# Expert results of a turn: one indirect scatter of 4 KB pieces where two of 2 KB stood

## What is computed

```python
def hier_moe(h, w_rg, w_re, w_gate, w_up, w_down):
    ...
    eid = g_top[:, None] * EXPERTS_PER_GROUP + top_i        # 2 of 16 experts for each token
    comb = jnp.sum(jax.nn.one_hot(eid, N_EXPERTS) * wts[..., None], axis=1)
    act = jax.nn.silu(jnp.einsum('nd,edf->nef', xf, w_gate)) * jnp.einsum('nd,edf->nef', xf, w_up)
    act = act * comb.astype(act.dtype)[..., None]
    return jnp.einsum('nef,efd->nd', act, w_down).reshape(b, t, dm)
```

## Time and profile before

| what | value |
|---|---|
| median of 3 runs | 1653.67 us (1653.02 to 1654.21) |
| the profiled execution's own time | 1659.17 us |
| its span, first to last instruction | 1657.3 us |
| TensorE's mean granted clock | 0.92 of full speed |
| PE busy | 1447.2 us, 87% |
| DVE busy | 387.6 us, 23% |
| ACT busy | 296.5 us, 18% |
| POOL busy | 83.2 us, 5% |
| DMA | 380.28 MB, mean 229 GB/s |

### The profile page before, as it was taken

The page is one execution under the profiler, slowest core; times in us unless marked ns, Lnnn a source line. Parts: engine busy times, 40 slices in busy tenths (PEclk is TensorE's granted clock), DMA queues, the critical chain, the costliest instruction groups (busy, mean ns, idle before and its releaser), DMA issues. The chain is left out here.

```text
span 1657.3 us, 19981 instructions
## 1 busy us (share of the span) xinstructions
PE 1447.2 (87%) x7384; PEld 790.8 (48%) x7385; DVE 387.6 (23%) x972; ACT 296.5 (18%) x667; POOL 83.2 (5%) x111
## 2 busy tenths in 40 slices
PE   7999999999999988878899999769999888797880
PEld 4444445556788756644454575433333223232330
DVE  3101010000365265466210213520101001010015
ACT  3000000011333234357100113100000000000001
POOL 0000000000200000000000000001010100101000
PEclk9999999999999689979899999969999889998995
DMA  9376224352242077400933123979999999999965
GB/s 356 112 306 241 102 99 132 105 173 102 102 153 64 23 219 235 149 13 1 356 117 122 82 102 107 403 271 389 391 415 387 396 408 408 416 412 405 417 294 194
DMA packets 113809, 380.28 MB, mean 229 GB/s; under 512 B 17459, under 2 KB 55387, under 8 KB 83047
## 3 DMA queue, kind: packets, MB, share of 16 engines
q1 hardware_dynamic: 108050, 343.27, 54.5%
q0 software_dynamic: 5552, 27.89, 4.9%
q10 hardware_dynamic: 144, 8.26, 1.2%
HBM read 394.60 MB, written 26.49 MB: 254 GB/s over the span
## 5 line engine op out<-in xcount | busy, mean ns | idle before, releaser
L2356 PE MATMUL bank<-ring,hT_e 128*64 x576 | 267.9, 626 | 56.2 <-DMA W<-in_w_exp_up 54.6
L2357 PE MATMUL bank<-W,hT_e 128*64 128x512 f32 x576 | 267.9, 626 | 0.0
L2356 PEld LDWEIGHTS bank<-ring,hT_e 128*64 128x64 f32 x576 | 82.0, 145 | 234.8 <-issue 234.8
L2373 PE MATMUL bank<-W,const 128*64 128x512 f32 x576 | 134.3, 621 | 9.8 <-ACT const L2401 9.8
L490 PE MATMUL bank<-raw,hT 128*128 128x512 f32 (+1 forms) x320 | 134.0, 581 | 0.6 <-PEq L243 0.6
L490 PE MATMUL bank<-w_in,hT 128*128 128x512 f32 (+2 forms) x320 | 123.7, 547 | 0.0
L1712 PE MATMUL bank<-W,mixT 128*128 128x512 f32 x256 | 113.4, 604 | 1.6 <-DVE mixT L1947 1.6
L490 PEld LDWEIGHTS bank<-raw,hT 128*128 128x128 f32 x320 | 62.4, 197 | 69.0 <-issue 68.7
L490 PEld LDWEIGHTS bank<-w_in,hT 128*128 128x128 f32 x320 | 60.4, 190 | 61.0 <-issue 60.9
L2419 DVE SCALAR_TENSOR_TENSOR gate<-bank,row_w,gate 64x512 f32<-64x512 f32 x18 | 13.6, 756 | 322.1 <-ACT gate L2399 322.1
L2373 PEld LDWEIGHTS bank<-W,const 128*64 128x64 f32 x576 | 42.7, 142 | 88.0 <-issue 88.0
(11 more groups left out here) (403 smaller groups left out, 1755.3 us busy)
## 6 DMA issues: line engine op xcount, KB each, us to landing
ring<-in_w_exp_gate SPq DMA_DIRECT2D x76, 1024.0 KB
W<-in_w_exp_down SPq DMA_DIRECT2D x76, 1024.0 KB, 29.3
W<-in_w_exp_up SPq DMA_DIRECT2D x72, 1024.0 KB
raw<-in_w_in SPq DMA_DIRECT2D x3, 4096.0 KB
W<-in_w_out SPq DMA_DIRECT2D x3, 4096.0 KB, 13.5
w_in<-in_w_in SPq DMA_DIRECT2D x2, 4096.0 KB, 14.7
k_in<-in_cache_sel_k SPq DMA_DIRECT2D x64, 128.0 KB
v_in<-in_cache_sel_v SPq DMA_DIRECT2D x64, 128.0 KB, 3.4
```

Source lines behind the costliest of these rows:

```text
L2356: pe.matmul(bank[4 + u][0:NS, :], hT[:, u, c, :], w_g[:, c, :], start=(c == 0), stop=(c == KC - 1))
L2357: mm = pe.matmul(bank[4 + u][UP, :], hT[:, u, c, :], w_u[:, c, :], start=(c == 0), stop=(c == KC - 1))
L2373: mm = pe.matmul(bank[2 * u + n // 2][lane, :], actT[:, q, :], w_d[:, u, q, 512 * n:512 * n + 512], start=(q == 0), stop=(q == 3))
```

## The change

The four 512-column quarters are placed otherwise in PSUM: n = 0 and 1 now lie on partitions 0 to 63 in the two banks, n = 2 and 3 on partitions 64 to 127. Each partition half then holds 1024 adjacent columns of the row in `y`, and one scatter of 128 pieces of 4 KB writes them. The scratch is viewed in rows of 1024 floats, the row numbers are 2 in place of 4 to a pair, the table `rows_at` loses a column, and the scatter's semaphore counts 16 a turn in place of 32. The place table `lane` loses its second column, so that the constants' row is 2950 floats wide in place of 2951.

```diff
-        "place1": np.stack([4 * ((k * TILES + r) * P + p) + 1 for r in range(TILES) for k in range(2)], 1),
+        "place1": np.stack([2 * ((k * TILES + r) * P + p) + 1 for r in range(TILES) for k in range(2)], 1),
-        "lane": np.stack([p // NS - 1, p // NS + 1], 1),
+        "lane": (p // NS - 1)[:, None],
...
-                    for h in range(2):
-                        dve.scalar_tensor_tensor(out=rows_at[:, :, 1 + h], in0=table[:, 1, :], scalar=cst("lane")[:, h:h + 1], in1=blank[:, :],
-                                                 op0=ALU.add, op1=ALU.add)
+                    dve.scalar_tensor_tensor(out=rows_at[:, :, 1], in0=table[:, 1, :], scalar=cst("lane"), in1=blank[:, :],
+                                             op0=ALU.add, op1=ALU.add)
...
-            y = const[:, P:P + 2048].rearrange("p (u h n) -> p u h n", u=2, h=2)
+            y = const[:, P:P + 2048].rearrange("p (u n) -> p u n", u=2)
...
-                    sp.wait_ge(y_stored, n * 64)
+                    sp.wait_ge(y_stored, n * 32)
...
-                    y_rows = scratch["moe_y"].rearrange("r (n c) -> (r n) c", c=512)
+                    y_rows = scratch["moe_y"].rearrange("r (n c) -> (r n) c", c=1024)
...
-                        pool.wait_ge(y_stored, turn * 32)
-                        pool.tensor_copy(to_row[:, u, :], rows_at[:, bass.ds(turn, 1), 1:3].rearrange("p o c -> p (o c)")).then_inc(to_ready, 1)
+                        pool.wait_ge(y_stored, turn * 16)
+                        pool.tensor_copy(to_row[:, u:u + 1], rows_at[:, bass.ds(turn, 1), 1]).then_inc(to_ready, 1)
...
-                        for h in range(2):
-                            pool.indirect_dma_start(out=y_rows, out_offset=bass.IndirectOffsetOnAxis(ap=to_row[:, u, h:h + 1], axis=0),
-                                                    in_=y[:, u, h, :], in_offset=None, bounds_check=8 * TILES * P - 1, oob_is_err=False).then_inc(y_stored, 16)
+                        pool.indirect_dma_start(out=y_rows, out_offset=bass.IndirectOffsetOnAxis(ap=to_row[:, u:u + 1], axis=0),
+                                                in_=y[:, u, :], in_offset=None, bounds_check=4 * TILES * P - 1, oob_is_err=False).then_inc(y_stored, 16)
...
-                            for n in range(4):
-                                lane = slice(NS * (n % 2), NS * (n % 2) + NS)
-                                mm = pe.matmul(bank[2 * u + n // 2][lane, :], actT[:, q, :], w_d[:, u, q, 512 * n:512 * n + 512], start=(q == 0), stop=(q == 3))
+                            for n in (0, 2, 1, 3):
+                                lane = slice(NS * (n // 2), NS * (n // 2) + NS)
+                                mm = pe.matmul(bank[2 * u + n % 2][lane, :], actT[:, q, :], w_d[:, u, q, 512 * n:512 * n + 512], start=(q == 0), stop=(q == 3))
...
-                        act.wait_ge(y_stored, turn * 32)
-                        act.copy(y[:, u, 0, :], bank[2 * u]).then_inc(y_copied_a, 1)
+                        act.wait_ge(y_stored, turn * 16)
+                        act.copy(y[:, u, 0:512], bank[2 * u]).then_inc(y_copied_a, 1)
...
-                        dve.wait_ge(y_stored, turn * 32)
-                        dve.tensor_copy(y[:, u, 1, :], bank[2 * u + 1]).then_inc(y_copied_d, 1)
+                        dve.wait_ge(y_stored, turn * 16)
+                        dve.tensor_copy(y[:, u, 512:1024], bank[2 * u + 1]).then_inc(y_copied_d, 1)
```

More of the change, by code:

```diff
@@ L1570, in trunk @@
         ahead = sb(top, "ahead", [1, TURNS_MAX + 2], I32)
-        rows_at = sb(top, "rows_at", [P, TURNS_MAX + 2, 3], I32)
+        rows_at = sb(top, "rows_at", [P, TURNS_MAX + 2, 2], I32)
         row_w = sb(top, "row_w", [P, TURNS_MAX + 2])
@@ L2241, in trunk @@
             from_row = side("from_row", [P, 2], I32)
-            to_row = side("to_row", [P, 2, 2], I32)
+            to_row = side("to_row", [P, 2], I32)
             to_ready = sem("e_to_ready")
```

## The result

The changed kernel is **slower**: its time against the kernel before is 1.0038 of it, 95% interval 1.0027 to 1.005, from 18 runs of each (medians 1663.49 and 1656.97 us). On the 1653.67 us of the forecast that is 6.3 us more, 1660.0 us. The forecast was 1652.4 us, with a range of 1650.6 to 1654.4.

The account below looks back on a forecast made before the run. The prediction took DMA engine time to bound the experts from 1120 to 1598 us. Scatters -0.2, POOL 0, router -0.15 and tail -0.95 summed to -1.3 us: 1653.67 to 1652.4 us, range 1650.6 to 1654.4.

Parts of the forecast that it names:

- What bounds the kernel: Experts, 1120 to 1598 us: all 16 DMA engines are full (busy share 1.01, 405 GB/s), so their time bounds this stretch.
- DMA engine time of the scatters: Scatters of all turns, 5120 KB: larger pieces save 0.2 us of DMA engine time, between 0 and 0.48.
- the upper end, 0: Scatters' DMA engine time: pieces travel one to a packet of 4 KB as now, so the gain is 0.
- The gather's price: Scatters' DMA engine time: at the gather's 63.4 ns a KB the scatters would cost 7.4 us more.
- POOL a turn: Each turn: gather issued 1.32 us earlier, landing 0 to 1.32 earlier; PE's 4.6 us of gather waits nearly vanish; time gain 0.
- Router's end: Router's end, before POOL's first gather: one of two L2231 instructions on DVE goes, -0.15 us.
- Tail: After DVE's last copy: one scatter issued 1.31 us sooner than the second, its doubled data 0.35 us longer, -0.95 us.
- PE, ACT, DVE in the turn: Within each turn: same steps, banks and copy shapes, SP waits for the same events, constants' row one float shorter: 0.
- The slower rival: DMA engines, 1120 to 1598 us: 4 KB pieces dearer or slowing loads beside them, 7.4 us longer, 1660.0 us; chance 0.05.
- my three signs of being wrong: Full stretch changes over 2 us; scatter leaves 38 to 41 ns a KB; last copy to reading back doesn't shrink 0.5 to 1.3.

## Why the prediction was wrong

*What bounds the kernel:* right. The experts are bound by DMA engine time from 1120 to 1598 us. The share is 1.01 in both kernels, and that is just why 0.7 ns a KB on the loads costs some 7 us.

*DMA engine time of the scatters, -0.2 us:* the number of packets and their price did not change (128 data packets, 40.2 and 40.0 ns a KB), so the upper end, 0, is the nearer one. The gather's price, the other bound, did not come in.

*POOL a turn, 0:* right in the sum, but the step's detail was not. The gather is issued 1.3 us earlier but lands 0.1 earlier, so PE's waits for it did not shrink to nearly nothing: they are 5.5 us, where they were 4.6. A gather delayed by 2.4 us cost nothing either.

*Router's end, -0.15 us:* `L2230` starts at 1085.80 and the next at 1085.96, 0.16 us where it was 0.31 for two.

*Tail, -0.95 us:* measured -0.94. The scatter is issued at 1619.55, 0.97 us after DVE's last copy, and lands after 2.68 us, 0.34 more than the second scatter before, against 0.35 taken.

*The step that failed* is in the part on DMA engine time and in the one that said "PE, ACT, DVE in the turn": the sum has a term for the scatters and none for the loads, whose 38.7 ns a KB it takes as the same in both kernels. It put them at nothing without a reason. I costed the instructions that the diff removes and the constants' row that gets shorter, and wrote of the table that loses a column without asking what is allocated behind it. The missing term is some +7 us: 183.5 MB of loads at 422 and not 429 GB/s. In the stage, the five kernels with both buffers off 256 need 530.7 to 535.0 us, the six runs with both on it 523.9 to 528.0 us, means 532.9 and 526.5, 6.4 us apart.

*The slower rival* named the place (the DMA engines between 1120 and 1598) and a time that came out right, 1660.0 us. Its mechanism is wrong: the pieces cost what they did, and the kernel with the pieces and without the move does not lose. A total that fits is no proof of the cause. Of my three signs of being wrong one came true, a full stretch longer by over 2 us, while the scatter stayed within 38 to 41 ns a KB and the tail shrank as forecast. It is just this pairing that led from the pieces to the loads.

## What stays open

The loss does not stand everywhere. In the changed kernel the loads of down matrices into the same misplaced `W` before the turns begin run at 426 and 428 GB/s, the rate of the buffers on 256 (windows from 1055 to 1065 us):

```profile
1055.00:1060.00 5.00, 1.56 (x11) 1.37 (x10) 3.54 (x8) 0.93 (x3) 0.00 (x0) 0.93 1.01 426
1060.00:1065.00 5.00, 4.92 (x54) 4.04 (x52) 2.52 (x5) 0.00 (x0) 0.00 (x0) 0.73 1.02 428
```

In the load-only windows read from 1245 us on it is 420 to 423. It comes gradually: of the 8 KB packets that start from 1140 to 1150 us 14% take more than 309 ns, from 1170 to 1180 us 78% (before: 5% and none). What has to come to the address for the loss to appear, and why a misplaced load pays less beside loads that start on 256, no run settles. Nor does any one ratio put the change's own gain beyond noise: four timings of the one scatter with the weights on 256 are 0.9978 to 0.9995, all below 1, and each interval holds 1. Of the forecast's 1.3 us the tail's part is seen in the profile, 3.67 us (last copy to reading back) in the changed kernel against 4.61; in all four the scatter lands 2.7 us after its issue, as there.

## What to carry to other kernels

A diff that changes the size of any buffer moves what is allocated behind it; print the start of the big DMA targets before and after, and keep them on multiples of 256 bytes. Where the DMA engines are full, look at the GB/s of a window that holds nothing but the bulk loads first: it tells in one row whether the bulk of the bytes got dearer. And on such a stretch saving issues on POOL gave only what the bare tail gave, here about 1 us.

## What the runs showed of the hardware

- Weight loads in 8 KB rows into buffers that all start 32, 64, 128 or 224 bytes above a multiple of 256 run at 419 to 423 GB/s in this stage's load-only windows, against 425 to 429 on 256, and from 1360 to 1378 us an 8 KB packet takes a mean of 313.7 to 314.7 ns against 309.0; a start on a multiple of 512 (427 GB/s) gives nothing more than one on 256.
- The loss of one misplaced load depends on the loads around it: 4.5 to 4.7 ns a packet where all weight loads are misplaced by 128 bytes, 0.9 ns for the gate loads alone and 2.5 ns for the down loads with the gate on 256.
- Two indirect pieces of 2 KB travel in one 4 KB packet, and a piece of 4 KB takes the same 159 ns; halving the number of pieces bought no DMA time.
- An indirect gather issued 2.1, 3.4 or 4.5 us behind a scatter lands 11.5, 11.6 and 12.2 us behind it (by medians) while the engines are full.
